# The first expert taken out of the expert loop, its first 128 rows gathered, turned and multiplied by themselves

## The reference, cut to what matters

```
p_group = jax.nn.softmax((t @ w_rg) + b_rg, axis=-1)
top_p, top_g = lax.top_k(p_group, 1)                  # one of 4 groups
top_l, top_e = lax.top_k(sel_logits, TOP_K_INNER)     # two of its 4 experts
gate = ...                                            # 0 for 14 of the 16 experts
y = jnp.zeros((b * s, d), F32)
for e in range(N_EXPERTS):                            # 16 experts
    a, u = jnp.split(t @ w_ei[e], 2, axis=-1)         # 1024 -> 2 x 512
    y = y + gate[:, e:e + 1] * ((jax.nn.silu(a) * u) @ w_eo[e])   # 512 -> 1024
```

## Time and profile before

| | |
|---|---|
| median of three runs | 1331.74 us |
| profiled execution | 1335.64 us |
| its span, first to last instruction | 1333.9 us |
| PE busy | 1262.2 us (95%) |
| DVE, ACT, POOL busy | 703.7, 621.8, 350.3 us |
| DMA | 212.34 MB, mean 159 GB/s |
| packets of queue q8 (kind instruction) | 51, 0.84 MB |

### The profile page before, as it was taken

How to read it: one execution, slowest core, us unless ns; L and a number is a source line. 1 busy time by engine, 2 the same in 40 slices (tenths; PEclk the granted TensorE clock), 3 DMA queues, 4 the chain that set the end, 5 groups by cost and what they waited for, 6 DMA issues and landing times. The chain is left out here.

```text
span 1333.9 us, 19178 instructions
## 1 busy us (share of the span) xinstructions
PE 1262.2 (95%) x7218; PEld 1037.6 (78%) x7219; DVE 703.7 (53%) x891; ACT 621.8 (47%) x845; POOL 350.3 (26%) x306
## 2 busy tenths in 40 slices
PE   8999999999999999999999999598999999989992
PEld 6888867788879888966788878476788888868871
DVE  5233367421476332266522475867854765775456
ACT  4222476522323222367522231766745665775445
POOL 0532000000120332000000120156653756575333
PEclk8999999999999999999999999688999999999996
DMA  6833200024363222200032553479977979898663
GB/s 221 282 121 96 64 1 2 32 95 141 112 253 126 96 95 96 94 1 2 9 113 79 179 168 148 154 247 314 309 263 223 301 240 296 259 347 274 179 203 134
DMA packets 63522, 212.34 MB, mean 159 GB/s; under 512 B 12390, under 2 KB 12902, under 8 KB 62647
## 3 DMA queue, kind: packets, MB, share of 16 engines
q1 hardware_dynamic: 49052, 178.24, 38.8%
q0 software_dynamic: 11808, 24.59, 7.1%
q10 hardware_dynamic: 2592, 8.53, 1.6%
HBM read 199.00 MB, written 34.25 MB: 175 GB/s over the span
## 5 line engine op out<-in xcount | busy, mean ns | idle before, releaser
L1509 DVE TENSOR_TENSOR wlo<-raw,whi 128x2048 fp32r<-128x2048 f32 (+1 forms) x51 | 113.7, 2230 | 175.6 <-ACT whi L1164 175.6
L1490 DVE TENSOR_TENSOR moe_lo<-moe_raw,moe_hi 128x2048 fp32r<-128x2048 f32 x81 | 185.1, 2306 | 32.8 <-ACT moe_hi L1338 32.3
L1338 ACT ACTIVATE moe_hi<-moe_raw 128x2048 fp32r<-128x2048 f32 x96 | 182.6, 1916 | 34.6 <-PE banks L741 20.1
L739 PE MATMUL banks<-xT,whi 128*128 128x512 f32 x448 | 175.8, 392 | 0.0
L740 PE MATMUL banks<-xT,whi 128*128 128x512 f32 x448 | 175.3, 391 | 0.0
L741 PE MATMUL banks<-xT,wlo 128*128 128x512 f32 x448 | 175.3, 391 | 0.0
L609 POOL TENSOR_TENSOR gated<-gated,kqv 128x512 f32<-128x512 f32 x16 | 25.3, 1597 | 489.9 <-DVE kqv L1656 489.9
L739 PE MATMUL banks<-moe_lo,xeh 128*128 128x512 f32 x368 | 146.9, 399 | 5.7 <-issue 4.1
L741 PE MATMUL banks<-moe_hi,xel 128*128 128x512 f32 x368 | 145.2, 395 | 0.0
L740 PE MATMUL banks<-moe_hi,xeh 128*128 128x512 f32 x368 | 145.1, 394 | 0.0
L1164 ACT ACTIVATE whi<-raw 128x2048 fp32r<-128x2048 f32 (+1 forms) x51 | 94.0, 1843 | 90.4 <-PE banks L741 84.8
(11 more groups left out here) (278 smaller groups left out, 2335.5 us busy)
## 6 DMA issues: line engine op xcount, KB each, us to landing
moe_raw<-in_expert_w SPq DMA_DIRECT2D x192, 512.0 KB
raw<-in_front_w SPq DMA_DIRECT2D x104, 512.0 KB, 4.9
toeplitz_rows<-bias_rows POOLq DMA_DIRECT2D x4, 1152.0 KB, 14.3
kqv<-in_x_turned SPq DMA_DIRECT2D x8, 512.0 KB, 7.7
pt<-in_x SPq DMA_DIRECT2D x2, 2048.0 KB, 9.2
x_rows<-pt ACTq DMA_DIRECT2D x8, 512.0 KB, 2.7
token_sums<-pt ACTq DMA_DIRECT2D x8, 512.0 KB, 3.6
moe_raw<-token_sums SPq DMA_DIRECT2D x8, 512.0 KB, 9.6
```

The source lines that it names most:

```text
L739: mm(dst, left[0], right[1], start=first, stop=False)
L1338: A(moe_hi[m % SPLIT_E], moe_raw[m % RAW_E], ACT.Copy).then_inc(e_hi, 1)
L1490: V.tensor_tensor(moe_lo[m % SPLIT_E], moe_raw[m % RAW_E], moe_hi[m % SPLIT_E].bitcast(F32), ALU.subtract).then_inc(lo_sem(m % ECH), 1)
L1509: V.tensor_tensor(view(lo, shape), view(raw[c % 2], shape), view(hi, shape).bitcast(F32), ALU.subtract).then_inc(w_split, 1)
```

## The change

The two gathers of expert 0 get a semaphore each, `first_in[0]` and `first_in[1]`. The four groups of transposes are cut anew, for all experts: a group is now four feature blocks of one half of the rows (`row_group`) and no longer two feature blocks of both halves, so that the groups 0 and 1 are the first 128 rows. Ahead of the first expert PE turns groups 0 and 1 when the first gather is in, multiplies chunk 0 with them, turns groups 2 and 3, and goes on. ACT puts the copies of groups 0 and 1 ahead of the high part of chunk 5, DVE puts its subtractions ahead of the low parts of chunks 4 and 5. On PE alone, experts 0 and 1 are written out in front of the loop, which now makes 6 trips.

```diff
+        first_in = [sem(f"first_in{c}") for c in range(2)]
...
             for b in range(2):
                 if b == 1:
-                    pool.wait_ge(rows_in[0], 32)
+                    for c in range(2):
+                        pool.wait_ge(first_in[c], 16)
...
-                        oob_is_err=False).then_inc(rows_in[b], 16)
+                        oob_is_err=False).then_inc(first_in[c] if b == 0 else rows_in[b], 16)
...
-            turn_rows(0, 0, 1, range(4), FIRST_BANKS)
-
-            def step(pair, b, width, more=True):
+            pe.wait_ge(first_in[0], 16)
+            for g in range(2):
+                turn_group(0, g, bank[FIRST_BANKS[g]])
+
+            def step(pair, b, width, more=True, first=False):
...
                     for r in range(width // P):
+                        if first and c < 2:
+                            pe.wait_ge(xe_lo, 2 + (c + 1 if r == 0 else 4))
...
+                        if first and c == 0 and r == 0:
+                            first_block = last
+                            pe.wait_ge(first_in[1], 16)
+                            for g in (2, 3):
+                                turn_group(0, g, bank[FIRST_BANKS[g]])
+                    (last if width > P or not (first and c == 0) else first_block).then_inc(e_used, 1)
+                    if first and c == 1:
+                        pe.wait_ge(xe_lo, 2 + 4)
...
-            with pe.Fori(0, last_pair) as pair:
+            either(0, 0, first=True)
+            either(0, 1)
+            with pe.Fori(1, last_pair) as pair:
                 for b in range(2):
                     either(pair, b)
...
+            rows_hi(0, 0, (0, 1), FIRST_BANKS)
             for c in range(RAW_E + 1, SPLIT_E):
                 e_split(0, c)
-            rows_hi(0, 0, range(4), FIRST_BANKS)
+            rows_hi(0, 0, (2, 3), FIRST_BANKS)
...
-            for c in range(2, SPLIT_E):
+            for c in range(2, RAW_E):
                 e_split(0, c)
-            rows_lo(0, 0, range(4), FIRST_BANKS)
+            rows_lo(0, 0, (0, 1), FIRST_BANKS)
+            for c in range(RAW_E, SPLIT_E):
+                e_split(0, c)
+            rows_lo(0, 0, (2, 3), FIRST_BANKS)
```

More of the change, by code:

```diff
@@ L464, in slot_gate, with row_group @@
             return scatter_ids[b].bitcast(F32)[:, SLOT_W * c + 1:SLOT_W * c + 2]
+        def row_group(t, g):
+            return t.rearrange("p (k n) -> p k n", k=KD)[:, 4 * (g % 2):4 * (g % 2) + 4, g // 2 * P:(g // 2 + 1) * P]
         def lo_sem(c):
@@ L670, in expert_dmas @@
                 pool.wait_ge(y_out[1 - b], pair * 32 + 32)
-                pool.wait_ge(rows_in[1 - b], pair * 32 + 32 + 32 * b)
+                pool.wait_ge(rows_in[1 - b], pair * 32 + 32)
                 bear(0).then_inc(y_gone, 1)
@@ L697, in _ @@
             pool.wait_ge(y_out[1], pair * 32 + 32)
-            pool.wait_ge(rows_in[0], pair * 32 + 32)
+            pool.wait_ge(rows_in[0], pair * 32)
             pool.wait_ge(scatter_ids_in[1], pair * 16 + 16)
@@ L1037, in _, with turn_group, turn_rows @@
             last_pair = pe.value_load(n_pass[0:1, 1:2], min_val=NE // 2 - 1, max_val=4 * (NE // 2) - 1)
-            def turn_rows(b, z, gathers, groups, banks=(2, 3, 2, 3)):
+            def turn_group(b, g, tb):
+                for q in range(4):
+                    c, k = g // 2, 4 * (g % 2) + q
+                    last = nc.tensor.transpose(tb[:, q * P:(q + 1) * P], x_rows[b][:, c * D + k * P:c * D + (k + 1) * P], ident)
+                last.then_inc(rows_T, 1)
+            def turn_rows(b, z, gathers, groups):
                 pe.wait_ge(rows_in[b], gathers * 32)
                 for g in groups:
[L1043 to L1050, removed]
-            turn_rows(0, 0, 1, range(4), FIRST_BANKS)
-            def step(pair, b, width, more=True):
+                    pe.wait_ge(xe_lo, z * 4 + g + 1)
+                    turn_group(b, g, bank[(2, 3, 2, 3)[g]])
+            pe.wait_ge(first_in[0], 16)
+            for g in range(2):
+                turn_group(0, g, bank[FIRST_BANKS[g]])
+            def step(pair, b, width, more=True, first=False):
                 z = pair * 2 + b
-                pe.wait_ge(xe_lo, z * 4 + 4 + 2)
+                if not first:
+                    pe.wait_ge(xe_lo, z * 4 + 4 + 2)
                 xv = [t.rearrange("p (k n) -> p k n", k=KD) for t in xe[b]]
@@ L1076, in rows_of_next @@
                     if more:
-                        turn_rows(1 - b, z + 1, pair + (1 if b == 0 else 2), groups)
+                        turn_rows(1 - b, z + 1, pair + 1, groups)
                 for c in range(XCH):
@@ L1088, in step @@
                                        [v[:, k] for v in w], kh == 0 and k == 0, kh == 1 and k == KD // 2 - 1)
-                    last.then_inc(e_used, 1)
+                        if first and c == 0 and r == 0:
[6 more added lines that the diff above has]
+                        pe.wait_ge(xe_lo, 2 + 4)
                     if c == 2:
@@ L1122, in step, with either @@
                     last.then_inc(e_used, 1)
-            def either(pair, b, more=True):
+            def either(pair, b, more=True, first=False):
                 full = pe.value_load(is_full[0:1, bass.ds(pair * 2 + b, 1)], min_val=0, max_val=1)
                 with pe.If(full < 1):
-                    step(pair, b, P, more)
+                    step(pair, b, P, more, first)
                 with pe.Else():
-                    step(pair, b, SLOTS, more)
-            with pe.Fori(0, last_pair) as pair:
+                    step(pair, b, SLOTS, more, first)
+            either(0, 0, first=True)
+            either(0, 1)
+            with pe.Fori(1, last_pair) as pair:
                 for b in range(2):
@@ L1356, in rows_hi @@
                     act.wait_ge(rows_T, z * 4 + g + 1 + 8)
-                    A(xe[b][0][:, g * 512:(g + 1) * 512], bank[banks[g]][:, :], ACT.Copy).then_inc(xe_hi, 1)
+                    A(row_group(xe[b][0], g), bank[banks[g]].rearrange("p (k n) -> p k n", k=4), ACT.Copy).then_inc(xe_hi, 1)
             for c in range(EARLY_E, RAW_E + 1):
@@ L1878, in rows_lo @@
                     dve.wait_ge(xe_hi, z * 4 + g + 1)
-                    V.tensor_tensor(xe[b][1][:, g * 512:(g + 1) * 512], bank[banks[g]][:, :],
-                                    xe[b][0][:, g * 512:(g + 1) * 512].bitcast(F32), ALU.subtract).then_inc(xe_lo, 1)
-            for c in range(2, SPLIT_E):
+                    V.tensor_tensor(row_group(xe[b][1], g), bank[banks[g]].rearrange("p (k n) -> p k n", k=4),
+                                    row_group(xe[b][0], g).bitcast(F32), ALU.subtract).then_inc(xe_lo, 1)
+            for c in range(2, RAW_E):
                 e_split(0, c)
-            rows_lo(0, 0, range(4), FIRST_BANKS)
+            rows_lo(0, 0, (0, 1), FIRST_BANKS)
+            for c in range(RAW_E, SPLIT_E):
+                e_split(0, c)
+            rows_lo(0, 0, (2, 3), FIRST_BANKS)
             dve.wait_ge(counted, 1)
```

## The result

Five runs of the changed kernel have a median of 1341.09 us (1338.9 to 1343.62), five of the kernel before 1332.44 (1330.62 to 1333.49): ratio 1.0061 [1.0048, 1.0075], 8.1 us slower by the ratio. The prediction had the sign and the two stalls, but 1336.3 us; its range ended at 1340.0. The profiled execution took 1342.3 us, span 1340.6, against 1335.64 and 1333.9.

What follows compares the result with a forecast made beforehand. PE was taken as the bound from expert 4 to 10, so microseconds won or lost before 959.39 us reach the end; -2.9 - 4.0 + 4.9 + 6.6 = +4.6 us gave 1336.3 us, range 1328.0 to 1340.0 (8 in 10).

Steps and rivals of the forecast that it cites:

- the sign: Whole kernel: slower, by 0.35%; chance of slower by over 0.2% put at 0.52.
- the two stalls: PE's jumps at the ends of experts 2 and 3 pass the fetched instruction block, replacing one stall before expert 2.
- The written-out experts: PE, experts 1 to 4: stall before expert 2 gone -4.0 us, stalls ending experts 2 and 3 +4.9 and +6.6.
- the clock that I priced on expert 3: Part of the +4.9 us for a stall at the end of expert 2: 2.5 us for the clock.
- rival 4: Three stalls, expert 1's jump too, landing 27 instructions before the fetched block's end: +8.6 us, 1340.3 us; chance 0.07.
- The start: Expert 0: first matmul 6.5 us earlier, gain limited by expert 1's second gather landing at 876.1: -2.9 us.
- the upper bound of 6.5: Expert 0's start: gain of 6.5 us at most if expert 1's second gather lands after 4.5 us, at 872.5.
- The bound of 4.0: Expert 0's start: gain of 4.0 us if chunk 1 is done only at 874.5.
- 0.9 us of landing: Expert 1's second gather: landing taken at 876.1 instead of 877.0, as later weight loads stand less in its way.
- The base: Profiled execution's 3.9 us over the median carried over as it is: 1331.74 + 4.6 = 1336.3 us.
- Rival 5: Expert 0's second gather brings almost nothing, the gain is only in not waiting; already in the sum, no chance given.
- Rival 3: Expert 1's gathers land by 873, start -5.5 instead of -2.9, one gap keeps the clock up: -0.5, 1331.2 us; chance 0.07.

Runs made afterwards that it cites:

- e1: Kernel before with only experts 0 and 1 written out in front of PE's loop, old start kept: 1339.2 us, 1.0057.
- e11: The changed kernel once more, a single execution: 1337.69 us.
- e7: Kernel before with expert 1's gathers issued early, POOL no longer waiting for those of expert 0: 1331.76 us, 0.9994.
- e2: Kernel before with 12 instead of 18 identity products at the start of PE's program, the rest 24 instructions earlier: 1330.44 us, 0.9984.
- e3: Kernel before with 24 instead of 18 identity products at the start of PE's program, the rest 24 instructions later: 1332.2 us, 1.0001.
- e8: Kernel before with 12 instead of 18 identity products at PE's start and expert 1's gathers issued early: 1330.67 us, 0.9983.
- e4: Changed kernel with 86 never-run transposes before the first transposes, the rest of PE's program 174 instructions later: 1332.68 us, 1.0.
- e5: Changed kernel with expert 1's gathers issued early, POOL no longer waiting for those of expert 0: 1333.58 us, 1.0014.
- e6: Changed kernel with the rest of PE's program 174 instructions later and expert 1's gathers issued early: 1328.42 us, 0.9973.
- e9: Changed kernel with expert 1's gathers issued early and the rest of PE's program moved by 40 instructions: 1336.29 us, 1.0025.
- e10: Changed kernel with expert 1's gathers issued early and the rest of PE's program moved by 126 instructions: 1332.44 us, 0.999.
- e12: Changed kernel without written-out experts, its loop over all pairs again and 16 transposes ahead of it: 1334.37 us, 1.0012.

## Why the prediction missed

**The written-out experts** (-4.0, +4.9, +6.6, together +7.5): right. e1 measures +7.6 [5.7, 9.3]. In the trace experts 1 and 2 together are 0.35 us longer, against -4.0 + 3.6 = -0.4; expert 3 is 4.52 longer against 2.5 - 1.2 + 4.05 = 5.35; expert 4 2.39 against 2.55. That the first three agree so well is in part luck: the clock that I priced on expert 3 fell in expert 2 (0.87, against 0.96 in expert 3), behind the 2.79 us for `hT`. Both branches stand on the line and at the experts named. Missed in them is the stop of 1.5 us in expert 2. Expert 1's jump lands 26 instructions before a border (rival 4 said 27); that is inside the fetched block, so there is no stall at the jump, but the packet of the next block comes only at 913.6, for a border reached at 914.6 (that it is asked for on landing is my reading). In this trace the gap behind expert 2, 0.68 us for the 3.6 I took, made that good; in e11 it was 3.33 us and did not.

**The start** (-2.9, "so the gain is 878.99 less the landing"): this is the step that failed. Its first half was right: first matmul 863.76 in e11 for the 864.1 forecast, `h_full` released by the landing of expert 1's second gather, 0.4 us behind it. What failed is to take the difference of the landings for the gain. Two things stand between the landing and the end of expert 0, and I priced neither.
1. The clock falls in the new wait. Expert 0 of the changed kernel has the granted clock at 0.50 from 877.7 to 884.5 us, from inside the wait of 4.25 us on, and a mean of 0.87. The 4 us won ahead of the wait are paid back in the wait, and the clock comes on top.
2. The same price was already in the execution that I started from. Its expert 0 ran at 0.90 and took 21.22 us, since the clock had fallen at 864.5 and came back only at 874.8. In e1's execution it came back at 867.6, and expert 0 took 19.69 us at a clock of 1.00 (row below) and ended at 889.5, against 889.9 in e11. Against that, the start gains nothing. Against the execution that I started from, e11 does gain what I forecast: `h_full` and the end of expert 0 both come 2.7 us earlier. So a gain over one slow execution was carried to the medians.

More traces say the same. From the issue of the first gather to the end of expert 0's last matmul it is 34.9 us in the kernel before and 35.4 in e7, whose clock was down for 10 us around the start of expert 0, but 32.7 to 33.6 us in e1, e2, e3 and e8, where it was down for 3.4. The new start with late gathers has 33.8 us (profiled above), 32.5 (e11) and 35.7 (e4), no better than the old one; with early gathers it has 28.0 to 29.1 us (e5, e6, e9, e10).

```profile
869.85:889.54 19.69, 19.27 (x93) 15.63 (x93) 9.83 (x11) 12.19 (x13) 13.17 (x11) 1.00 0.65 231
```

e5 settles it from the other side: with the gathers early, 6.3 us come back. Over e1, which has the written-out experts and the old start, that is a gain of 5.7 us, near the upper bound of 6.5 that I had worked out for a landing that does not matter. (The bound of 4.0 beside it is wrong: 877.9 less 874.5 is 3.4. It enters no sum.) I had that bound, and argued over 0.9 us of landing (less in the queue's way), where the term that mattered was the issue: 868.0 us in the earlier trace rows, 862.5 in e5.

**The base.** I carried over that the profiled execution lay 3.9 us over the median as it was. That of the changed kernel lies 1.2 over. The difference of the two traces, 6.7 us, includes 1.7 us of scatter at the first gather, and the medians differ by 8.65. The miss of 4.8 us on the time is 3.4 from the start (-2.9 for +0.5; how much of it is the stop in expert 2, which e1 lacks, no run shows), 0.1 from the written-out experts, and the rest, 1.3, from medians that scatter between sets of runs; e1's profiled execution even lies 3.3 us under its own median.

**The rivals.** Rival 4 was nearest in time (1340.3) but not by its mechanism; that is e9, where the jump of expert 1 really passes the block. Rival 5, that the second gather brings nothing and the gain is only in not waiting for it, changes nothing in the sum, as it says. Rival 3 had the right lever, the landing of expert 1's gathers by 873, but nothing in this kernel pulls it: POOL waits for both gathers of expert 0 first.

## What to carry to other kernels

Before you let an engine start earlier, list what it will wait for next and who issues that: moving the start without the next transfer moves idle time, and here the clock fell in it as well. Before you carry a gain from a trace to the medians, see whether the stage that it comes from ran in that execution as it does in others. Code written out of a loop is not free even if it does the same work; compare the long branches and the instruction packets of both traces, and try the same program some tens of instructions earlier or later before you judge an edit by less than 1%. A difference below that in one pair of traces is scatter until the medians show it.

## What the runs showed of the hardware

- A jump of PE that by my count leaves the block fetched ahead makes its branch 3.3 to 6.4 us long instead of 0.17, and PE idles 1.1 to 2.6 us less than that: 5.34 and 4.05 in the kernel before, 3.28 and 0.68 and then 6.03 and 4.95 in the changed one, 5.25 and 3.05 in e9. A block that by the count was next, but came late, costs 1.6 (e12) to 4.7 us of branch and between 0 (e5, 1.99 us at 882.4) and 2.7 us of PE. The sizes overlap, so it is the count that tells the two kinds apart. The Trainium skill ("Runtime: NRT & Kernel Launch", Instruction fetch mechanics) has prefetch sequential and a stall where a taken branch leaves a window of two pages. The long branches agree with the stall; the window as written does not, for a loop of some 1,130 instructions fetches nothing between 970 and 1240 us, here as in the earlier trace rows. The same section gives PE a store of 2048 instructions, which fits that.
- Shifting a program by instructions that never run moved the time by 8.1 us (e4 against the changed kernel), as much as the whole change had cost.
- The granted clock fell to its lower level, 1.2 of 2.4 GHz, inside idle stretches of PE: from 915.7 to 922.6 us in the kernel before (4.05 us idle ahead of 917.28), from 877.7 to 884.5 and from 928.9 to 935.7 us in the changed one (4.25 us ahead of 879.34, 2.79 ahead of 929.54), from 876.4 to 879.8 us in e11 (3.91 us ahead of 877.03). Through the 1.02 us ahead of 952.35 in the kernel before it stayed up.
- Four gathers in a row did not slow each other much: in e5 the first took 4.4 us, as in the earlier trace rows (4.5), the second 7.0 (6.7 in the kernel before), and expert 1's 8.6 and 8.2 us (8.5 and, in the earlier trace rows, 9.0 in the kernel before).
